# Head sums of squares as two products of rounded parts, and one rotation product on GpSimd, in a two-block transformer kernel

## The reference, cut to what matters

```
# first block, layer 1: dilated attention, 3 groups x 8 heads of 64
q = partial_rope(rms_norm(q, q_norm), cos, sin)     # norm over the 64 channels of a head
k = partial_rope(rms_norm(k, k_norm), cos, sin)     # rotates the first 16 channels of a head
...
# second block, the mixer
q = rms_norm_2(aq, q_norm);  k = rms_norm_2(ak, k_norm);  ik = rms_norm_2(ik, idx_k_norm)
ya = dsa_attention(q, k, v, iq, ik, iw)             # top-128 keys by an index score
yb = mlstm_branch(...)                              # ends in a norm over 128 channels per head
```

## Time and profile before

| | |
|---|---|
| median of three runs | 1865.81 us |
| the profiled execution | 1860.73 us |
| its span | 1858.7 us |
| PE busy | 1803.4 us, 97% of the span |
| ACT busy | 1132.2 us, 61% |
| DVE busy | 900.8 us, 48% |
| POOL busy | 315.4 us, 17% |
| chain that ended last | PE 78%, DVE 15%, ACT 4% |
| `sum_squares` (line 1806) | 84 matmul instructions (42 sums), 592 ns median each |

### The profile page before, as it was taken

The page is one execution under the profiler, slowest core; times in us unless marked ns, Lnnn a source line. Parts: engine busy times, 40 slices in busy tenths (PEclk is TensorE's granted clock), DMA queues, the critical chain, the costliest instruction groups (busy, mean ns, idle before and its releaser), DMA issues.

```text
span 1858.7 us, 24263 instructions
## 1 busy us (share of the span) xinstructions
PE 1803.4 (97%) x8915; PEld 1419.5 (76%) x8915; DVE 900.8 (48%) x1588; ACT 1132.2 (61%) x1548; POOL 315.4 (17%) x409
## 2 busy tenths in 40 slices
PE   6999899999999889999999999999999999999999
PEld 4877687777777678888888876767766888888887
DVE  5999557656657564222211165696464432222100
ACT  6687858666656476555554475666565565556443
POOL 1222012322222011111111111011100111111111
PEclk9999999999999999999999999999999999999999
DMA  8899688865565277888889976446743888888897
GB/s 237 192 211 203 170 202 198 195 155 133 139 142 135 87 170 188 199 191 193 197 203 230 228 179 158 114 113 138 162 121 91 210 189 196 197 192 197 200 215 191
DMA packets 94039, 328.05 MB, mean 176 GB/s; under 512 B 12416, under 2 KB 12544, under 8 KB 93184
## 3 DMA queue, kind: packets, MB, share of 16 engines
q0 software_dynamic: 47440, 158.36, 46.5%
q1 hardware_dynamic: 43920, 157.57, 25.8%
q10 hardware_dynamic: 2592, 10.94, 1.6%
HBM read 162.45 MB, written 6.29 MB: 91 GB/s over the span
## 4 chain that ended last, share of the span: by engine, by line
PE 78%; DVE 15%; ACT 4%; issue 2%; DMA 1%; ACTq 0%; DVEq 0%
PE ps L1731 67%; DVE cv_acc L1293 3%; DVE tmp L1293 3%; PE ps L1748 2%; PE ps L1806 1%; DMA w_lo<-w_raw 1%; PE ps L2240 1%; DVE rs L1108 1%; DVE rs L1109 1%; PE ps L2025 1%; DVE rs L1107 1%; ACT at_Sm L837 1%; DVE at_Sm L1396 1%; PE ps L1767 1%; PE ps L2013 0%
## 5 line engine op out<-in xcount | busy, mean ns | idle before, releaser
L1731 PE MATMUL ps<-H_hi,w_hi 128*128 128x512 f32 x1272 | 510.0, 401 | 8.5 <-DMA w_lo<-w_raw 6.3
L1731 PE MATMUL ps<-H_hi,w_lo 128*128 128x512 f32 x1272 | 496.1, 390 | 0.0
L1731 PE MATMUL ps<-H_lo,w_hi 128*128 128x512 f32 x1272 | 495.7, 390 | 0.0
L482 POOL DMA_DIRECT2D w_lo<-w_raw x289 | 250.0, 865 | 1352.6 <-ACT w_lo L561 1319.4
L547 ACT ACTIVATE w_hi<-w_raw 128x1024 fp32r<-128x1024 f32 x292 | 306.3, 1049 | 121.7 <-PE ps L1731 120.7
L561 ACT ACTIVATE w_lo<-w_raw 128x1024 fp32r<-128x1024 f32 x292 | 304.6, 1043 | 0.0
L1731 PEld LDWEIGHTS ps<-H_hi,w_hi 128*128 128x128 f32 x1272 | 239.2, 188 | 68.9 <-issue 15.3
L1731 PEld LDWEIGHTS ps<-H_lo,w_hi 128*128 128x128 f32 x1272 | 239.3, 188 | 55.9 <-issue 7.2
L1731 PEld LDWEIGHTS ps<-H_hi,w_lo 128*128 128x128 f32 x1272 | 239.0, 188 | 50.3
L1147 DVE SCALAR_TENSOR_TENSOR X<-ps,X 128x512 f32<-128x512 f32 (+1 forms) x36 | 27.0, 751 | 252.9 <-PE ps L1731 245.3
L1731 PE MATMUL ps<-mid_hi,w_hi 128*128 128x512 f32 x352 | 136.9, 389 | 0.0
(11 more groups left out here) (367 smaller groups left out, 2751.9 us busy)
## 6 DMA issues: line engine op xcount, KB each, us to landing
w_raw<-weights SPq DMA_DIRECT2D x292, 512.0 KB, 4.6
w_lo<-w_raw POOLq DMA_DIRECT2D x289, 512.0 KB, 5.4
cv_yl<-cv_a POOLq DMA_DIRECT2D x8, 256.0 KB, 3.3
pl_P<-spill ACTq DMA_DIRECT2D x1, 2048.0 KB, 8.5
spill<-X ACTq DMA_DIRECT2D x8, 256.0 KB, 5.2
X<-spill ACTq DMA_DIRECT2D x2, 1024.0 KB, 6.6
out<-X SPq DMA_DIRECT2D x8, 256.0 KB, 4.9
at_C<-cv_Y POOLq DMA_DIRECT2D x7, 256.0 KB, 8.6
```

The lines of the kernel that those rows point to most:

```text
L482: pool.dma_start(w_lo[:, u, :], w_raw[:, u, :], accum_op=ALU.add).then_inc(lo_landed[u], 16)
L1731: mm = pe.matmul(ps[:, bank, :], w, x, start=first and n == 0 and q == 0, stop=last and n == len(blocks) - 1 and q == 2, skip_group_check= ...
```

## The change

24 head sums in stage 4 and 5 ("c") in stage 9 change form; the four "h" sums, the indexer's one and the eight of the layer norm stay.

```
@@ ACT: squares
+            def square_parts(src, sq_hi):
+                act.wait_ge(sq_used, k.at(sq_done))
+                act.activation(sq_hi[:, :], src, ACT.Square)
+                act.activation(sq[:, 0, :], src, ACT.Square).then_inc(sq_done, 1)
@@ ACT, start of stage 4
+            copy(head_ones_r[:, :], head_ones).then_inc(con_rounded, 1)
@@ ACT, stage 4 / stage 9
-                            square(raw)
+                            square_parts(raw, at_sq)
-                    square(dsa_chunk(HEAD_SUMS[s_ + 1][1])[0])
+                    square_parts(dsa_chunk(HEAD_SUMS[s_ + 1][1])[0], mx_sq)
@@ DVE
+            def square_low(sq_hi):
+                dve.wait_ge(sq_done, k.up(sq_done))
+                dve.tensor_tensor(sq_lo[:, :], sq[:, 0, :], sq_hi[:, :].bitcast(F32), ALU.subtract).then_inc(sq_low, 1)
@@ DVE, stage 4 (behind the masked maximum) / stage 9 (behind ml_h and the diagonals)
+                    if c < 4 and j in SUM_SLOT:
+                        square_low(at_sq)
+                if HEAD_SUMS.get(s_, "h")[0] == "c":
+                    square_low(mx_sq)
@@ DVE, rotation
-                        dve.wait_ge(pair_loaded[n % 2], 64 * (3 * c + n // 2 + 1))
-                        dve.tensor_tensor(pair, pair, odd, ALU.mult)
+                        dve.wait_ge(pair_made, len(QK_TILES) * c + n + 1)
@@ PE
+            def sum_parts(bank, lhsT, sq_hi):
+                pe.wait_ge(sq_low, k.up(sq_low))
+                pe.matmul(ps[:, bank, :], lhsT[:, :], sq_hi[:, :], start=True, stop=False)
+                pe.matmul(ps[:, bank, :], lhsT[:, :], sq_lo[:, :], start=False, stop=True).then_inc(sq_used, 1)
@@ PE, before the first tile of stage 4
+            pe.wait_ge(con_rounded, 1)
@@ POOL, stage 4
+            def turn(n):
+                odd = (at_S[:, :], at_T[:, 1, :])[i % 2]
+                pool.wait_ge(pair_loaded[n % 2], 64 * (n // 2 + 1))
+                pool.tensor_tensor(at_pair[:, n % 2, :], at_pair[:, n % 2, :], odd, ALU.mult).then_inc(pair_made, 1)
                     low(first + SLOTS * c + j)
+                    if j - 1 in QK_TILES:
+                        turn(len(QK_TILES) * c + QK_TILES.index(j - 1))
```

More of the change, by code:

```diff
@@ L174, in build @@
         H_hi, H_lo = scope(("H_hi", [P, KC, S], F32R), ("H_lo", [P, KC, S], F32R))
-        yb_hi, yb_lo, ds_P, ds_PT, ds_acc = scope(
+        yb_hi, yb_lo, ds_P, ds_PT, ds_acc, mx_sq = scope(
             ("yb_hi", [P, 4, S], F32R), ("yb_lo", [P, 4, S], F32R), ("ds_P", [P, 2, S], F32), ("ds_PT", [P, 2, S], F32),
-            ("ds_acc", [P, 9 * P], F32))
+            ("ds_acc", [P, 9 * P], F32), ("mx_sq", [P, S], F32R))
         sb("H_room", [P, 2 * KC, S])
@@ L183, in build @@
         con = sb("con", [P, NCONST])
+        head_ones_r = sb("head_ones_r", [P, P], F32R)
+        _, sq_lo = scope(("sq_0", [P, S], F32), ("sq_lo", [P, S], F32R))
         sq = sb("sq", [P, 2, S])
@@ L215, in build @@
                                 ("rp", [P, 5, S], F32))
-            (at_raw, at_pair, at_mask, at_T, at_SG, at_Sm, at_PT, at_Yh, at_Yl, at_V, at_st) = scope(
+            (at_raw, at_pair, at_mask, at_T, at_SG, at_Sm, at_PT, at_Yh, at_Yl, at_V, at_sq, at_st) = scope(
                 ("at_raw", [P, 12, S], F32), ("at_pair", [P, 2, S], F32), ("at_mask", [P, 4, S], F32),
@@ L262, in build @@
         sq_done = sem("sq_done")
+        sq_low = sem("sq_low")
+        pair_made = sem("pair_made")
+        con_rounded = sem("con_rounded")
         sq_used = sem("sq_used")
@@ L576, in square @@
                 k.up(sq_done)
+            def square_parts(src, sq_hi):
+                act.wait_ge(sq_used, k.at(sq_done))
+                act.activation(sq_hi[:, :], src, ACT.Square)
+                act.activation(sq[:, 0, :], src, ACT.Square).then_inc(sq_done, 1)
+                k.up(sq_done)
+                k.up(sq_low)
             def logs():
@@ L1384, in _ @@
             k.up(gated, 4)
+            k.up(sq_done, k.at(sq_used))
             for c in range(5):
@@ L1430, in _ @@
                         raw, pair = at_raw[:, 6 * (c % 2) + n, :], at_pair[:, n % 2, :]
-                        even, odd = ((at_C[:, :], at_S[:, :]), (at_T[:, 0, :], at_T[:, 1, :]))[n % 2]
-                        dve.wait_ge(pair_loaded[n % 2], 64 * (3 * c + n // 2 + 1))
-                        dve.tensor_tensor(pair, pair, odd, ALU.mult)
+                        even = (at_C[:, :], at_T[:, 0, :])[n % 2]
+                        dve.wait_ge(pair_made, len(QK_TILES) * c + n + 1)
                         link(dve.tensor_tensor(raw, raw, even, ALU.mult))
@@ L1615, in _ @@
                     instr.then_inc(diag_done, 1)
+                if HEAD_SUMS.get(s_, "h")[0] == "c":
+                    square_low(mx_sq)
+                elif s_ in HEAD_SUMS:
+                    k.up(sq_done)
                 if s_ == 14:
@@ L1802, in pair @@
                 k.up(read_out)
+            def sum_parts(bank, lhsT, sq_hi):
+                k.up(sq_done)
+                pe.wait_ge(sq_low, k.up(sq_low))
+                pe.matmul(ps[:, bank, :], lhsT[:, :], sq_hi[:, :], start=True, stop=False)
+                pe.matmul(ps[:, bank, :], lhsT[:, :], sq_lo[:, :], start=False, stop=True).then_inc(sq_used, 1)
+                k.up(sq_used)
             def sum_squares(c, n, bank=4, lhsT=None):
@@ L2085, in _ @@
                             pe.wait_ge(v_copied, GROUPS * c + (j == 4))
-                        sum_squares(0, 1, 1, head_ones)
+                        sum_parts(1, head_ones_r, at_sq)
                     if c < 4 and j == SLOTS - 1:
@@ L2255, in _ @@
                         pe.wait_ge(v_copied, V0 + MH + 1)
-                    sum_squares(0, 1, 7, None if HEAD_SUMS[s_][0] == "h" else head_ones)
+                    if HEAD_SUMS[s_][0] == "h":
+                        sum_squares(0, 1, 7)
+                    else:
+                        sum_parts(7, head_ones_r, mx_sq)
                     k.up(rs_done)
```

4 lines of the change are left out of this document (3 added, 1 removed).

## The result

The changed kernel takes 1895.7 us (median of 4 runs, 1888.3 to 1896.5) where the kernel before takes 1863.1 (4 runs beside it). The ratio is 1.0162, interval 1.0140 to 1.0185: slower by 30 us (32.5 between the medians), and outside the range of the prediction. The kernel before takes either about 1860 or about 1866 us from one execution to the next, so a median of few runs moves by some us with the mix, and a difference is given by the ratios wherever the two disagree.

What follows compares the result with a forecast made beforehand. PE, busy 97% of the span, was taken as the bound. Stage 4 steady -11.9, its start +6.1, mixer +1.6, clock +0.8 gave -3.4, rounded to -3: 1857.7 us, or 1862.5 as a median, range 1852 to 1871.

Steps and rivals of the forecast that it cites:

- the cost of GpSimd's product: Stage 4: the product moved to GpSimd was taken to fit in time, under 1.9 us, at cost 0.
- get in each other's way: Rival, 13%: GpSimd's product slows VectorE by up to 0.7 us twice per chunk; +4, net about 0, median 1866.
- VectorE rows longer than 0.69 us beside POOL's: Sign listed as showing the prediction wrong: VectorE operations in the profile after lengthened beside GpSimd's product.
- GpSimd's length: Stage 4: GpSimd's product taken as under 1.9 us, bounded by 0.69 us below and 3.35 us above.
- the estimate of 1.3: Stage 4: by the skill page, GpSimd needs about 1.3 us for the product's 512 elements; sum unchanged.
- The 6 us for a first call: Chunk 0, by the skill page: a routine's first call costs about 6 us, first product 2.7 late, sum up about 2.
- The gain per sum and the steady chunks: Each sum 0.41 us cheaper, 9.8 us over stage 4's 24; with waits in chunks 1 to 3, -11.9 us.
- Stage 4's start: PE waits for the copy of head_ones_r: 4.2 us lost, plus 1.9 for a lowered clock; +6.1 us.
- The mixer: Five sums gain 2.1 us, new waits 0.7 (step 3) and 3.4 (step 6), 0.4 goes: +1.6; clock +0.8.
- A late product: Rival, 14%: GpSimd's product takes longer than about 1.9 us and delays VectorE's rotation in stage 4; +6, median 1872.
- new sums no cheaper: Rival, 6%: each new sum needs a mode switch or weight load that shows; +6, median 1872.
- the gain standing: Rival, 22%: clock not lowered after stage 4's idle start, mixer's VectorE less late; -8.5 us, median 1857.

Runs made afterwards that it cites:

- e2: Kernel before with only the rotation's first product moved to GpSimd, the sums as they were; 1878.1 us, ratio 1.0083.
- e3: Changed kernel with PE's wait for the rounded head_ones moved from stage 4's start to just before the first sum; 1885.6 us, ratio 1.0126.
- e4: Changed kernel with the product back on VectorE and PE's wait before the first sum, leaving the new sums; 1865.5 us, ratio 1.0010.
- e1: Changed kernel with only the rotation's first product put back on VectorE; 1869.8 us, ratio 1.0034.
- e13: e11 with GpSimd's product ahead of its at_pair fetches, released by its tile's sum and VectorE's rotation before; 1852.7 us, ratio 0.9953.
- e10: e3 with GpSimd's product waiting for PE's sum of the same tile, ahead of the fetch of weights; 1868.6 us, ratio 1.0028.
- e5: e4 with VectorE making the mixer's difference for a chunk's sum ahead of the operations ending in ml_h; 1865.6 us, ratio 1.0006.
- e6: e3 with the product on VectorE and a GpSimd operation of one SBUF source in its place; 1884.7 us (one run).
- e11: e10 with the mixer's five chunk sums as before the change; 1866.5 us, ratio 1.0014.
- e14: Kernel before with only GpSimd's product added, timed as in e13, with the old sums; 1858.8 us, ratio 0.9968.
- e7: e3 with GpSimd's product made to wait until VectorE has made var of the same tile; 1867.9 us, ratio 1.0028.
- e9: e3 with GpSimd's product cut into four pieces of 128 columns; 1878.6 us (one run).
- e12: e4 with the mixer's sums as before, leaving only stage 4's new sums, product on VectorE; 1860.5 us, ratio 0.9985.

## Why the prediction was wrong

**The step that failed** is the cost of GpSimd's product, taken as nothing, and priced in the rival "get in each other's way" at 0.7 us twice per chunk, 4 us in all, with 13%. The mechanism was the rival's, its size was not. A row that meets the product loses up to 1.9 us (2.61 less 0.69; once, through two products, 4.1), not the product's 0.7 on VectorE, and 23 of the 24 products meet one. Against a product on VectorE it costs 15.5 us alone (e2) and 22 to 24 beside the new sums (e3 less e4, changed kernel less e1), lower clock included. The prediction's term, though, is a product that costs nothing on either engine, and e13 has it nearly so: e3 is 32 us above e13, of which 3 to 5 are the mixer's new sums. That leaves 27 to 29 us for this single term, and turns -3 into +24 to +26, for +30 measured. The small rest is within the intervals of these ratios; the two terms that may hold it are below. The prediction's own list of what would show it wrong had this sign, VectorE rows longer than 0.69 us beside POOL's.

The Trainium skill ("SBUF — State Buffer", section "SBUF: two separate sides") says that VectorE and GpSimd share a pair of SBUF ports as an exclusive lock held for the whole instruction, and that the other "fully blocks"; on VectorE's side it names instructions in a two-port mode and those with two SBUF inputs. (The scaling has one input in SBUF, so it would be of the first kind; no run here tells.) The prediction used the milder sentence of another page and priced a slowdown. The rows here agree with the lock: a wait until the product's end, and 0.30 or 0.56 us behind it. The page also gives the pair to whoever starts first. Six products of e10 bear that out: GpSimd had stood idle before them, the VectorE row that had begun 0.14 to 0.46 us ahead kept its 0.69 us, and the product took 1.39 to 1.71 us in place of 1.30. Where the product directly follows a DMA issue of GpSimd's, as in the changed kernel, rows that began up to 0.52 us ahead (525.85 is 0.42 ahead) were held all the same. That the DMA issue already counts as the start would fit, and no run here tests it.

**GpSimd's length**, under 1.9 us: right, but for one row of 1.96. It was 1.58 to 1.67 in the others, whose rows begin 0.2 to 0.35 us before the DMA issue ahead of them is over, and 1.28 to 1.31 where GpSimd is free (nearly all of e13, and most of e10, with held VectorE rows beside them or not); the estimate of 1.3 from the page cited in the prediction fits the second. The 6 us for a first call, by the same page, did not show: the first product (338.28) starts 0.2 us before the DMA issue ahead of it ends, and takes 1.62.

**The gain per sum and the steady chunks** (-3.16 us a chunk): right once the hold is away. From its first matmul to the one behind the wait for `at_Yl`, e13's stage 4 takes 319.8 us for 330.7, 10.9 less where 11.9 were forecast, and of that chunk 0, put at nothing, gives back a wait of 0.4 for its difference. In e13 the same wait recurs after 75.07 us, where the kernel before took 78.19 (481.57 in the earlier trace rows and the first row here, which is of the kernel before):

```profile
559.76 0.66 PE L2025 MATMUL ps<-con,at_Sm 128*128 128x128 f32 x4 [0.28 <-DVE at_Sm L1409]
```
```profile
439.63 0.66 PE L2070 MATMUL ps<-con,at_Sm 128*128 128x128 f32 x4 [0.32 <-DVE at_Sm L1444]
514.70 0.66 PE L2070 MATMUL ps<-con,at_Sm 128*128 128x128 f32 x4 [0.32 <-DVE at_Sm L1444]
```

**Stage 4's start** (+6.1): right. The wait came at 5.91 us. The clock was at half from 316.4 to 323.2, 6.8 us, but PE was idle for the first 1.9 of them; from its start at 318.29 twelve matmuls took 5.13 us where 2.72 is their full speed, so 2.4 were lost where 1.9 was taken, within the bounds of 0 to 3. (The expectations of e3 and e4 halve the whole stretch and so take too much.) e3 gave 7 us back by the ratios.

**The mixer** (+1.6, clock +0.8): waits 0.70 and 3.09 us for the 0.7 and 3.4 forecast, and the clock did fall behind the second, by an estimate 2.4 us lost for the 0.8 taken (half of PE's busy time at 1255 to 1262 us). The mixer's cost was 3 us in one pair of kernels and 5 in the other, for 2.4 forecast. e5 adds what the prediction did not see: the order of VectorE's work there can't be mended by one move.

**The other rivals.** A late product, new sums no cheaper, and the gain standing were all not what happened: no wait of VectorE names `at_pair` or POOL in the changed kernel, and the sums cost their 0.46 us.

## What to carry to other kernels

Work moved to GpSimd was not off VectorE's path here: ask which VectorE instruction each piece will meet, and give it a place beside instructions that read PSUM, by a semaphore and by its order among GpSimd's own DMAs. The same product was worth 15 us of loss or 6 of gain by its place alone. Where a price is taken as nothing because no row shows it, and a rival names a reason for one, measure that first: it was 27 us here. A shorter stream on the bounding engine pays only as far as the next engine's period, here 8.65 us a slot, so look at that period before summing the gains.

## What the runs showed that was not expected

- VectorE's scaling (one input in SBUF, 0.49 us) and its operations with two inputs in SBUF are held; those with one in PSUM (var, the maximum, the value tile) and rows of 128 x 1 are not. In e13 all 24 products meet var, and each var is 0.69 us.
- Who is held depends on what GpSimd did before. Behind a DMA issue its product held rows begun up to 0.52 us ahead; out of idleness it waited for the row itself (e10).
- PE's clock fell behind waits of 2.0 to 2.3 us in chunks 0, 2 and 3 of the changed kernel. It stayed at 1.00 behind one of 3.31 us there (ended 465.11), and behind the 1.68 us at the start of stage 4 in e3; in e3 it fell behind the same wait as the first (3.30 us, ended 455.59). What decides is open. Each of the four such stretches in chunks 0, 2 and 3 was 3.4 us at half clock, so 1.7 us lost on top of the gap.
- The kernel before itself falls in two groups, near 1860 us at a mean granted clock of 0.994 or 0.995, and near 1866 at 0.991 or 0.992. In the profiles of the changed kernel, e1, e2, e4, e5, e6, e11 and e14 there is a stretch at half clock at 176 to 180 us, ahead of anything the change touches, the next, near 230, is twice as long (6.8 us for 3.4), and stage 4 begins some 3 to 4 us later than in those of before, e3, e7, e9, e10, e12 and e13. All but the changed kernel and e1, which wait there anyway, have a third one of 3.4 us near 320. The three add 10.2 us at half clock, some 5 us lost, which is about the distance of the two groups and of their clocks. What sets the first one off is open; no profile of the kernel before from the upper group was taken.
